# A hybrid decoder layer in split fp32: another order and another share of the work at the entry to the up projection, and 32 sample rows that move one place forward and are multiplied as high and low side by side

## The reference, cut to what matters

```python
x = x + rmsnorm(merged @ w_out, g_mix_post)
up = rmsnorm(x, g_ffn_pre) @ ffn_w_up            # 1024 -> 2 * 2816
ext = jnp.concatenate([conv_hist, up], axis=1)
c = ffn_conv_b
for j in range(CONV_W):
    c = c + ext[:, j: j + T] * ffn_conv_w[j]
act = jax.nn.gelu(c[..., :D_FF], approximate=True) * c[..., D_FF:]
x = x + rmsnorm(act @ ffn_w_down, g_ffn_post)
```

## Time and profile before

| | us |
|---|---|
| median of 3 runs | 1572.86 (1572.39 to 1578.10) |
| the profiled execution | 1574.93 |
| its span, first to last instruction | 1573.2 |
| PE busy in the span | 1525.0 (97%) |
| DVE, ACT, POOL busy | 896.0, 584.6, 293.2 |
| mean granted TensorE clock | 0.978 of full |

### The profile page before, as it was taken

One profiled execution on the slowest core, in us unless ns is written; L12 is line 12 of the kernel. 1 busy time (PEld: TensorE's weight loads), 2 busy tenths in 40 slices (PEclk: granted clock), 3 DMA queues, 4 the chain that ended last, 5 costly groups with the idle time before them and its releaser, 6 DMA issues.

```text
span 1573.2 us, 26849 instructions
## 1 busy us (share of the span) xinstructions
PE 1525.0 (97%) x10067; PEld 1416.9 (90%) x10067; DVE 896.0 (57%) x1548; ACT 584.6 (37%) x1084; POOL 293.2 (19%) x290
## 2 busy tenths in 40 slices
PE   7999999999999999999996999999999999999997
PEld 7889999999999999997876999999999998888875
DVE  6575564666332232226565777777777775554644
ACT  7233232333222122124443444454434444453432
POOL 1124143340100000000104333333333320000000
PEclk9999999999889999999996999999999999999999
DMA  7134455451332441303203666556662238665471
GB/s 258 58 109 138 136 176 189 138 153 34 111 111 73 118 121 56 121 14 134 84 31 118 215 200 218 194 185 218 215 225 74 72 97 300 238 210 180 154 244 67
DMA packets 145809, 227.65 MB, mean 145 GB/s; under 512 B 14011, under 2 KB 116441, under 8 KB 144831
## 3 DMA queue, kind: packets, MB, share of 16 engines
q1 hardware_dynamic: 136711, 203.97, 40.6%
q0 software_dynamic: 8736, 22.08, 3.8%
q10 hardware_dynamic: 288, 0.59, 0.1%
HBM read 196.46 MB, written 74.34 MB: 172 GB/s over the span
## 4 chain that ended last, share of the span: by engine, by line
PE 91%; DVE 4%; DMA 2%; ACT 2%; issue 1%; POOL 1%; SPq 0%; ACTq 0%; DVEq 0%
PE PS L1313 28%; PE PS L1134 19%; PE PS L1379 13%; PE PS L1029 9%; PE PS L1272 6%; PE PS L1010 4%; PE PS L1198 2%; PE PS L1086 2%; PE PS L1058 1%; PE PS L1374 1%; PE PS L1072 1%; PE PS L1242 1%; PE PS L991 1%; DMA as_stage<-acts 1%; PE PS L1042 1%
## 5 line engine op out<-in xcount | busy, mean ns | idle before, releaser
L1313 PE MATMUL PS<-h_lo,wr_hi 128*128 128x264 f32 x1056 | 217.2, 286 | 0.0
L1313 PEld LDWEIGHTS PS<-h_lo,wr_hi 128*128 128x128 f32 x1056 | 166.1, 190 | 0.0
L1313 PE MATMUL PS<-t_hi,wr_hi 128*128 128x264 f32 x704 | 150.4, 293 | 4.4 <-DVE wr_lo L2273 3.4
L2336 DVE TENSOR_TENSOR wd_lo<-wd_stage,wd_hi 128x1024 fp32r<-128x1024 f32 x66 | 80.8, 1225 | 118.0 <-ACT as_hi L1749 117.8
L1313 PE MATMUL PS<-h_hi,wr_hi 128*128 128x264 f32 x704 | 145.4, 288 | 1.9 <-DVE xb L2233 1.4
L1313 PE MATMUL PS<-t_hi,wr_lo 128*128 128x264 f32 x704 | 145.9, 287 | 0.0
L2007 DVE TENSOR_TENSOR tw_lo<-tw_stage,tw_hi 128x1024 fp32r<-128x1024 f32 (+1 forms) x28 | 32.6, 1166 | 177.8 <-ACT tw_hi L1523 177.5
L1748 ACT ACTIVATE wd_hi<-wd_stage 128x1024 fp32r<-128x1024 f32 x66 | 69.9, 1059 | 130.5 <-PE PS L1379 76.6
L1313 PEld LDWEIGHTS PS<-t_hi,wr_hi 128*128 128x128 f32 x704 | 111.5, 192 | 5.2 <-issue 3.5
L1134 PE MATMUL PS<-hT_hi,tw_hi 128*128 128x352 f32 x480 | 112.1, 344 | 1.7 <-issue 1.6
L1313 PEld LDWEIGHTS PS<-h_hi,wr_hi 128*128 128x128 f32 x704 | 108.8, 189 | 5.1 <-DVE xb L2233 1.6
(11 more groups left out here) (320 smaller groups left out, 3430.4 us busy)
## 6 DMA issues: line engine op xcount, KB each, us to landing
wd_stage<-in_ffn_w_down SPq DMA_DIRECT2D x66, 512.0 KB, 3.5
tw_stage<-in_ffn_w_up SPq DMA_DIRECT2D x88, 256.0 KB, 5.0
out_k_s<-in_cache_k_w SPq DMA_DIRECT2D x8, 2044.0 KB
out_v_s<-in_cache_v_w SPq DMA_DIRECT2D x8, 2044.0 KB
qb<-zs SPq DMA_DIRECT2D x24, 512.0 KB, 5.1
acts<-cact POOLq DMA_DIRECT2D x22, 528.0 KB, 9.6
tw_stage<-in_w_in SPq DMA_DIRECT2D x20, 512.0 KB, 5.7
as_stage<-acts SPq DMA_DIRECT2D x44, 192.0 KB, 3.8
```

Source lines behind the costliest of these rows:

```text
L1313: last = pe.matmul(PS[:, bank + b, 0:BH], w[slot][:, k, :], x[:, k, b * BH:(b + 1) * BH], start=(k == 0 and j == 0), stop=(k == HK - 1 and ...
L2336: dve.tensor_tensor(wd_lo[slot][:, :], wd_stage[slot][:, :], wd_hi[slot][:, :].bitcast(F32), ALU.subtract)
```

## The change

The 32 sample rows move from the last place to the last but one (place 7; `SMALL`). Their low part is no longer a third pass: it is written beside the high part (32 columns each), so one pass with the high weights multiplies both at once (64 rows out) and one pass with the low weights the high part alone. DVE adds the two halves of the output afterwards (`fold`: a copy and an addition), and ACT's Square, DVE's scaling of this tile then read the sum from `row` instead of PSUM.

At the entry: the four `ws_sum` go from DVE to POOL; POOL clears `chist` behind them, ahead of the `t_lo`. Of the eight `t_lo`, POOL makes block 0 of product 6 and both of product 4, DVE the five others (before: DVE four, POOL four). ACT splits block 0 of products 4 and 5 before it waits for the last tile. PE takes `turn_out(8)` ahead of block 0 of product 6, and product 2 waits for the scaling of the last tile instead of its addition.

```diff
-ORDER = (0, 4, 1, 5, 2, 6, 3, 7, 8)
+ORDER = (0, 4, 1, 5, 2, 6, 3, 8, 7)
+SMALL = ORDER.index(8)
...
+            for i in HALF_TILES[:3]:
+                second_half(i)
+            pool.wait_ge(x2_out, 16 * 7 + U0)
+            pool.wait_ge(hn_ready[1], 7)
+            sums(0)
+            pool.wait_ge(o_mm, 9 + 2)
+            pool.memset(chist[:, :, :], 0.0).then_inc(pool_set, 1)
+            low_t(1, 2, 0)
+            second_half(HALF_TILES[3])
+            second_half(HALF_TILES[4])
+            low_t(3, 4, 0)
+            low_t(7, 4, 1)
...
+                if i == SMALL:
+                    for k in range(KC):
+                        passes = ((2 * TS, wo_hi), (TS, wo_lo))
+                        for j, (both, w) in enumerate(passes if k < KC - 1 else passes[::-1]):
+                            for b in range(2):
+                                last = pe.matmul(PS[0:both, 2 * (i % 2) + b, :], mg_hi[i % 2][:, k, 0:both], w[:, k, b * 512:(b + 1) * 512],
+                                                 start=(k == 0 and j == 0), stop=(k == KC - 1 and j == 1))
+                    last.then_inc(o_mm, 1)
+                    return
...
                 if first:
-                    pe.wait_ge(o_x2, 9 + 2)
+                    pe.wait_ge(o_step, 2 * NTILE + 2)
                 else:
                     pe.wait_ge(c_out, f * 7 + U0)
                 product(2, q + 1, slot[1], 0).then_inc(p_done, 1)
                 if first:
+                    turn_out(8)
+                    pe.wait_ge(t_sums, TS0 + 4)
+                    product(6, q + 2, slot[2], 4, (0,))
+                    pe.wait_ge(u_out, U0 + 1)
                     pe.wait_ge(t_lo_done, U0 + 1)
-                    product(6, q + 2, slot[2], 4, (0,))
-                    turn_out(8)
-                    pe.wait_ge(u_out, U0 + 1)
+                    product(7, q + 3, slot[3], 2, (0,))
                     pe.wait_ge(t_lo_done, U0 + 2)
...
-                    pe.wait_ge(t_sums, TS0 + 7)
+                    pe.wait_ge(t_sums, TS0 + 8)
...
-                    pe.wait_ge(t_sums, TS0 + 9)
+                    pe.wait_ge(t_lo_done, U0 + 5)
...
+            split_t(4, 0)
+            split_t(1, 0)
             act.wait_ge(ht_done[1], 9 + 2)
-            act.wait_ge(t_sums, TS0 + 5)
-            for n, b in ((2, 1), (3, 1), (4, 0), (4, 1), (1, 0), (1, 1)):
-                split_t(n, b)
+            split_t(2, 1)
+            act.wait_ge(t_sums, TS0 + 6)
+            for n in (3, 4, 1):
+                split_t(n, 1)
...
+            def fold(i):
+
+                dve.wait_ge(o_mm, i + 1 + 2)
+                dve.wait_ge(ht_turned[1], i + 2)
+                flat = PS[0:2 * TS, 2 * (i % 2):2 * (i % 2) + 2, :].rearrange("p b n -> p (b n)")
+                dve.tensor_copy(row[0:TS, :], flat[TS:2 * TS, :]).then_inc(o_step, 1)
+                dve.wait_ge(o_step, 2 * i + 1)
+                dve.tensor_tensor(row[0:TS, :], flat[0:TS, :], row[0:TS, :], ALU.add).then_inc(o_step, 1)
...
+            dve.wait_ge(t_sums, TS0 + 6)
+            low_t(5, 2, 1)
+            low_t(6, 3, 1)
+            low_t(4, 1, 0)
+            low_t(8, 1, 1)
```

More of the change, by code:

```diff
@@ L535, in build @@
         t_step, t_hi_done, t_lo_done, x2_out = a_scored, a_pT_lo, a_pv, a_pT
+        HALF_TILES = [i for i, n in enumerate(ORDER) if n * P + P > HALF]
         t_sums, TS0 = a_pT_hi, 2 * NU
@@ L913, in _ @@
             pool.dma_start(ats, oacc[:, :]).then_inc(ats_out, 16)
[L915 to L929, removed]
             def sums(f):
@@ L1670, in post_norm @@
                     act.wait_ge(ht_turned[1], i + 2)
-                act.activation(row[0:rows, :], PS[0:rows, 2 * (i % 2):2 * (i % 2) + 2, :].rearrange("p b n -> p (b n)"), ACT.Square,
-                               accum_out=pss[0:rows, 0, n:n + 1]).then_inc(o_ss, 1)
+                psum, summed_ = PS[0:rows, 2 * (i % 2):2 * (i % 2) + 2, :].rearrange("p b n -> p (b n)"), row[0:rows, :]
+                if n == 8:
+                    act.wait_ge(o_step, 2 * i + 2)
+                    psum, summed_ = summed_, psum
+                act.activation(summed_, psum, ACT.Square, accum_out=pss[0:rows, 0, n:n + 1]).then_inc(o_ss, 1)
                 act.wait_ge(o_ss, i + 1)
@@ L2227, in residual @@
                 dve.reciprocal(prstd[0:rows, 0, n:n + 1], prms[0:rows, 0, n:n + 1]).then_inc(o_step, 1)
-                dve.wait_ge(o_step, i * 2 + 1)
-                dve.scalar_tensor_tensor(row[0:rows, :], PS[0:rows, 2 * (i % 2):2 * (i % 2) + 2, :].rearrange("p b n -> p (b n)"),
+                steps_ = i * 2 + (2 if i >= SMALL else 0)
+                dve.wait_ge(o_step, steps_ + 1)
+                product = PS[0:rows, 2 * (i % 2):2 * (i % 2) + 2, :].rearrange("p b n -> p (b n)") if n < 8 else row[0:rows, :]
+                dve.scalar_tensor_tensor(row[0:rows, :], product,
                                          prstd[0:rows, 0, n:n + 1], gpost[0:rows, :], ALU.mult, ALU.mult).then_inc(o_step, 1)
-                dve.wait_ge(o_step, i * 2 + 2)
+                dve.wait_ge(o_step, steps_ + 2)
                 dve.wait_ge(x_in[i % 4], 16 * (i // 4 + 1))
@@ L2279, in summed @@
                 low_weights(f * 7 + place, (7 * r + place) % 4, ws_sum[n - 1][:, :, :])
[L2281 to L2294, removed]
-                    dve.tensor_tensor(ws_sum[3][:, :, :], x12, ws_sum[1][:, :, :], ALU.subtract).then_inc(w_sum, 1)
             def low_t(count, n, b):
@@ L2303, in _ @@
             for i in range(NTILE):
+                if i == SMALL:
+                    fold(i)
                 residual(i)
@@ L2307, in _ @@
                 if i == 8:
[L2308 to L2309 removed]
+                    out_turned(7)
                 renorm(i)
[L2311 removed]
+                if 0 < i < 8:
                     out_turned(i - 1)
@@ L2315, in _ @@
                     quarter(0, 0, 0, 1, 1)
-                    dve.wait_ge(x2_out, 16 * 7 + U0)
-                    sums(0, (1, 3))
+            summed(0, 0, 2, 2)
             low_t(2, 3, 0)
```

20 lines of the change are left out of this document (13 added, 7 removed).

## The result

The changed kernel takes 1567.49 us (median of 7 runs, 1564.68 to 1569.93), the kernel before in the same comparison 1575.25 us (7 runs): ratio 0.9948, 95% interval 0.9933 to 0.9964, so 8.2 us less (5.7 to 10.6). A later comparison gave 0.9951 [0.9938, 0.9964] for the same pair. In the profiled executions the spans are 1573.2 and 1564.0 us.

A forecast was written before the change was run, and what follows sets the result against it. The entry is bound by POOL's and DVE's rows, not memory. Product 4 at 840.4 plus 8.5 and 1.1 us gives 850.0, 9.3 before 859.27; subtracted from the median 1572.86 this gives 1563.6 us, range 1559.5 to 1568.0.

The forecast's parts named there:

- rival 2: Sample chain: POOL goes first throughout, all four weight sums fall on it, 3.4 us more, product 1 later; 1567.0; chance 0.13.
- rival 3: Clock falls around 812 us; products 1, 2 and both blocks 0 at half speed, 8.5 us more; 1567.9; chance 0.12.
- the queue: Sample chain: scalings with two SBUF operands wait for POOL; first scaling and addition lose about 0.8 and 1.0 us.
- rival 1: Sample chain: scalings don't queue behind POOL, product 4 some 2.1 us earlier; 1561.5; chance 0.20.
- my sign for it: Sample chain: each scaling taking 2 us or more shows queueing behind POOL; 1.28 us shows none.
- Rival 4: Side-by-side tile lowers the clock at 799, last tile's 48 matmuls run at half, 11.2 us more; 1574.8; chance 0.05.
- 1.2 of the sample part's 3.6 us: Up to product 1: shorter sample tile gains 3.6 us, of which 1.2 is left; start 814.8 instead of 816.00.
- the sign that I named for rival 3: PE's windows: a granted clock of 0.50 before 824 us.
- The stop of 0.9 that I had there: Behind products 1 and 2: PE stands 0.9 us for the last tile's scaling, done at 821.5; transposes to 822.3.
- the clock in products 4, 5 and 3: 72 matmuls, 8.5 us at full clock; half clock costs between 0 and 2.9 us more, 1.1 taken.

The follow-up runs named there:

- the share alone: The changed kernel with the sample tile in 48 matmuls and no fold: 1566.93 us, 0.9946 of the kernel before.
- its relative: The changed kernel with the regrouped tail, but sample rows in 48 matmuls and no fold: 1561.00 us, 0.9911 of the kernel before.
- the early clearing: The kernel before with only the clearing of `chist` moved forward on POOL, ahead of its four low parts: 1570.34 us, 0.9976.
- the sample part alone: The kernel before with only the sample rows last but one, 32 matmuls and the fold: 1572.61 us, 0.9991.
- the share alone again: Second run of the changed kernel with the sample tile in 48 matmuls and no fold: 1569.60 us, 0.9963 of the kernel before.

## Why the prediction came out as it did

**Right overall; the size a little high.** It had 9.3 us; the profiles of the change show 10.46 (76.89 - 66.43) and 8.16 (76.89 - 68.73) on the way, and the comparisons of medians 8.2 and 7.7 us. The forecast of 1563.6 us itself lies 3.9 below the median measured. 2.4 of that is the starting point: the three runs known beforehand had a median of 1572.86, in the comparison it is 1575.25. The other 1.5 is the gain, 7.8 by medians instead of 9.3. I had given 0.64 to a median below 1565.0, and that did not come. The median lies nearer to the times of rivals 2 and 3 (1567.0 and 1567.9) than to the forecast; what tells them apart is the trace.

**Front.** The sample tile takes 7.64 us (793.36 to 801.00; 7.5 forecast). The scaling and the addition lose 0.64 and 0.97 us to POOL (0.8 and 1.0), and the run without POOL there gives these back, so the queue is shown, and rival 1 is out; but my sign for it, 2 us or more for each scaling, was set too high. The second scaling came behind POOL's last sum without waiting for it: POOL ended at 812.53, and the scaling, released by ACT, began at 813.10 and took 1.27. It ends at 814.37, 812.97 on the old axis (812.9). Product 1 is at 814.85 there (814.8): rival 2 is out. Rival 4 is out too: the side-by-side tile ran at 1.00 (window from 792.50). Of the 51 instructions that I gave as its counterpart before, 48 are matmuls of 32 columns and three the end of the transposes ahead of them; the clock of that window was 1.00 all the same. The Trainium skill ("SBUF — State Buffer", section "Who interferes with whom") says that a VectorE instruction with two SBUF inputs contends with a GpSimd instruction that reads SBUF; for the scaling, which no row of before could show, 1.91, 1.69 and 1.68 us beside POOL against 1.27 without agree.

**That 1.2 of the sample part's 3.6 us would be left.** Product 1 came 1.0 us earlier with the product side by side than without it, and in time it is worth about 1 us, which the runs do not part from nothing. Right at product 1; the change's gain is nearly all its share-out of work (0.9946 and 0.9963 alone).

**Middle.** The last tile's scaling ends at 822.86, on the old axis 821.46 (821.5), but its transposes start only at 822.33, where I had them start at 821.5 and end at 822.3. PE does not stand before them, though I had 0.9 us: products 1 and 2 took 7.5 us instead of the 6.1 that they took with the sums on DVE (820.15 - 0.89 - 813.12), because of the new stretch at 0.50. This is the sign that I named for rival 3. Its place was right and its price too high: I had both products and both blocks 0 at half speed, 4.3 us of it reaching the end; the stretch was 3.4 us long. The stop of 0.9 that I had there took up part of it, and DVE hid the 0.9 us by which the transposes were late: it had a low part and split weights to make until 825.76 and took the tile out right behind them (825.68). The second time the stretch was 6.8 us long, PE's transposes came 1.1 us later than the first time, and DVE stood 0.8 us for them.

**Tail.** One low part 3.47 and 3.49 (3.6); the last of the six ends at 837.98 on the old axis (838.4); block 1 of product 6 at 832.28 (832.7), its wait 6.0 us by DVE; product 4 at 839.92 (840.4). All six exclude one another, as said: they took 9.30 us (830.08 to 839.38), where 9.8 is the sum of what they take alone.

**The term that was mis-sized** is the clock in products 4, 5 and 3, 1.1 us of the 9.6 forecast for their 72 matmuls. The first execution lost nothing to the clock there (850.18 - 841.32 = 8.86 us, all at 1.00), the second ran 3.4 us of product 4 at 0.50 and took 10.3 (860.32 - 8.82 - 841.21). It is not one number but differs from execution to execution, and with the early stretch it spreads the way by 2.3 us. The forecast lies about in the middle of the two, which is luck: I had taken it from the 1.0 us that the kernel before lost, and had not seen that it would vary.

What sets off the early stretch stays open. The change and its relatives, where PE stood 1.1 to 1.2 us twice around the sample transposes, had it in all five profiles, 3.4 or 6.8 us long, from 812.3 to 816.8. With a stop of 0.8 us ahead of product 1 and one of 0.9 behind product 2 (weight sums on DVE), or with no stop ahead of product 1 (the share alone and its relative), none of five had 0.50 before 827; nor had the kernel before, the early clearing or the sample part alone, where PE stood 1.4 to 2.6 us between products 1 and 2. No run changed the stops alone.

## What to carry to other kernels

When a load is the last link of a wait, look at what else is late just under it: taking away 10 us of wait gave 3.8, because POOL's row kept PE standing 4.5 us in its place and more of product 4 then ran at 1.2 GHz. Work given to POOL is not free time on DVE while both read SBUF: what counted here was the sum of both engines' instructions in that stretch (9.3 us for six low parts that take 9.8 one by one), so POOL should get what lies in DVE's gaps, and the tail ahead of a waiting PE should be the few operations that its next product needs, in that order. And after a change that makes PE stand elsewhere, read the granted clock again: a start of product 4 that came 1.3 us earlier was worth nothing where the first 6 us from there ran at 1.2 GHz.

## What the runs showed of the hardware that I had not expected

The spread from run to run has a place. With the same work ahead of them, the transposes of place 5 came between 789.53 and 794.41 us in these profiles, in step with the stretches at half clock from 340 to 600 us: counted from the granted clock in windows of 2 us, they are 37.5 us in all in the earliest, 41 in the kernel before, 47.8 in the change and 51.2 in the two latest. Two windows show it. The first is that of the earliest, POOL's last low parts on DVE, the second that of the share alone again (794.38):

```profile
340.00:600.00 260.00, 253.18 (x1812) 249.71 (x1813) 97.38 (x199) 69.35 (x94) 12.02 (x19) 0.93 0.34 97
```

And the second:

```profile
340.00:600.00 260.00, 253.31 (x1781) 249.94 (x1782) 96.90 (x198) 67.05 (x91) 12.20 (x20) 0.90 0.33 96
```

PE is as busy in both, and the second has 31 matmuls fewer in its records, at a mean clock of 0.90 against 0.93. The 4.9 us between these two executions lie there, hundreds of us ahead of the change, and what sets them off is not shown: so a stretch is to be measured from a point just ahead of it.
